# Weights, states and cached keys in contiguous runs, and four places for weights in a hybrid decoder step

## The reference, cut to what matters

```python
h = _rmsnorm(x, norm_mix_w)
z, xbc, dt_raw, q, kv_c, kv_s, kv_w, nsa_g, br_g = _split_proj(h @ w_in)       # 1024 x 8016 or so columns
y_ssm, conv_new, ssm_new = _mamba_branch(z, xbc, dt_raw, conv_prev, ssm_prev, ...)
o_attn, win_new = nsa_core(q, kv_c, kv_s, kv_w, gates)                         # compressed, selected, window
g = sigmoid(br_g)
merged = g[..., :D] * (y_ssm @ w_ssm_branch) + g[..., D:] * (o_attn @ w_attn_branch)
x = x + merged @ w_out
x = x + _peer_tokens(_rmsnorm(x, norm_ffn_w), peer_wq, peer_sub_keys, peer_u, peer_v)

# _causal_conv, inside _mamba_branch: width 4 over 3072 channels, with the last 3 inputs as state
xp = concatenate([conv_prev, xbc], axis=1)
conv_new = xp[:, -(CONV_WIDTH - 1):]
# _ssd: chunks of 128 tokens, a state of 32 heads x 64 x 128 carried from chunk to chunk and returned
# _peer: q = h @ peer_wq; scores against peer_sub_keys; 128 experts a token, one row of peer_u and of peer_v each
act = gelu(einsum('nd,nhkd->nhk', h, peer_u[experts]))
y = einsum('nhk,nhkd->nd', g * act, peer_v[experts])
```

## Time and profile before

| | before |
|---|---|
| time, three runs | 3235.7, 3231.45, 3214.28 us; median 3231.45 us |
| the profiled execution | 3234.93 us, of which the span of the profile is 3233.2 us |
| granted clock of TensorE, mean | 0.811 |
| busy time of TensorE (matmuls) | 2217.7 us, 69% of the span |
| busy time of VectorE | 1543.3 us, 48% |
| busy time of ScalarE | 616.9 us, 19% |
| busy time of GpSimd | 1492.6 us, 46% |
| read from HBM | 821.54 MB |

### The profile page before, as it was taken

How to read it: one execution, slowest core, us unless ns; L and a number is a source line. 1 busy time by engine, 2 the same in 40 slices (tenths; PEclk the granted TensorE clock), 3 DMA queues, 4 the chain that set the end, 5 groups by cost and what they waited for, 6 DMA issues and landing times. The chain is left out here.

```text
span 3233.2 us, 32111 instructions
## 1 busy us (share of the span) xinstructions
PE 2217.7 (69%) x11116; PEld 1403.4 (43%) x11116; DVE 1543.3 (48%) x3888; ACT 616.9 (19%) x1746; POOL 1492.6 (46%) x1509
## 2 busy tenths in 40 slices
PE   8999979869777678756688894653446777564044
PEld 7788846556555466422235362332114443111000
DVE  4410042276888751256520065998535665108720
ACT  3330053113331100013340012321001111000000
POOL 0200000053254664457754357657555665443775
PEclk9999969879978888877899996655668898777567
DMA  6234602437637997889989978968988998997998
GB/s 218 79 92 121 140 26 78 130 111 236 204 102 257 332 325 263 266 325 350 350 308 290 349 250 287 352 221 284 412 344 325 352 389 304 314 340 288 339 370 316
DMA packets 401016, 843.89 MB, mean 261 GB/s; under 512 B 71194, under 2 KB 236914, under 8 KB 398181
## 3 DMA queue, kind: packets, MB, share of 16 engines
q0 software_dynamic: 170912, 644.95, 54.6%
q1 hardware_dynamic: 229944, 196.89, 20.4%
HBM read 821.54 MB, written 24.33 MB: 262 GB/s over the span
## 5 line engine op out<-in xcount | busy, mean ns | idle before, releaser
L3314 POOL DMA_INDIRECT e_ring<-in_peer_u,e_idx x576 | 692.2, 1202 | 542.9 <-DVE e_dot L3463 267.4
L3463 DVE CUSTOM_DVE_ANT_0 e_ring<-e_ring,e_h 128x1024 f32<-128x1024 f32 x576 | 703.0, 1254 | 175.4 <-DMA e_ring<-in_peer_u,e_idx 82.4
L3314 POOL DMA_INDIRECT e_ring<-in_peer_v,e_idxT x576 | 583.4, 1013 | 440.3 <-PE ps L3381 178.1
L3381 PE MATMUL ps<-e_ring,e_wz 128*32 128x512 f32 x2304 | 361.5, 742 | 297.1 <-DMA e_ring<-in_peer_v,e_idxT 261.3
L3381 PEld LDWEIGHTS ps<-e_ring,e_wz 128*32 128x32 f32 x2304 | 76.8, 125 | 507.2 <-issue 502.4
L1672 POOL CAST ra_atf<-ra_at 128x32 f32<-128x32 uint32 x8 | 1.7, 211 | 259.7 <-DVE ra_hit L1665 259.7
L379 PE MATMUL ps<-hTb,wb 128*128 128x320 f32 x384 | 112.1, 447 | 1.9 <-DMA wb<-in_w_in 1.9
L1957 PE MATMUL ps<-ss_bsel,ss_xde 64*128 64x512 f32 x64 | 54.6, 947 | 63.1 <-DVE room L2007 27.5
L1004 PE MATMUL ps<-hTb,wb 128*128 128x320 f32 x256 | 77.3, 462 | 16.9 <-DMA wb<-in_w_in 9.6
L379 PEld LDWEIGHTS ps<-hTb,wb 128*128 128x128 f32 x384 | 73.7, 197 | 30.8 <-issue 2.9
L1507 DVE TENSOR_REDUCE apb_nmax<-ps 128x2 f32<-128x768 f32 (+1 forms) x32 | 34.9, 1089 | 105.9 <-PE ps L1431 55.3
(11 more groups left out here) (720 smaller groups left out, 4329.9 us busy)
## 6 DMA issues: line engine op xcount, KB each, us to landing
wb<-in_w_in SPq DMA_DIRECT2D x38, 1024.0 KB, 5.3
e_ring<-in_w_in SPq DMA_DIRECT2D x24, 1024.0 KB, 5.3
wb<-in_peer_wq SPq DMA_DIRECT2D x10, 1024.0 KB, 5.4
wb<-in_w_ssm_branch SPq DMA_DIRECT2D x9, 1024.0 KB, 6.1
e_ring<-in_peer_u,e_idx POOLq DMA_INDIRECT x576
e_ring<-in_peer_v,e_idxT POOLq DMA_INDIRECT x576
e_ring<-in_w_ssm_branch SPq DMA_DIRECT2D x7, 1024.0 KB, 5.8
wb<-in_w_in SPq DMA_DIRECT2D x24, 256.0 KB, 4.3
```

What stands on the lines that cost most here:

```text
L3314: nc.gpsimd.indirect_dma_start(out=self.ring[:, place % self.NR, :], out_offset=None, in_=k.peer_u if kind == "u" else k.peer_v, in_offset ...
L3381: last = nc.tensor.matmul(k.ps[32 * b:32 * b + 32, self.SUMS + i, :], self.wz[:, at:at + 32], self.ring[:, self.v_at[n] % self.NR, 512 * i ...
L3463: v.tensor_tensor_reduce(uu, uu, self.h[:, tile % 2, :], 1.0, 0.0, ALU.mult, ALU.add, self.dot[:, tile % 2, t:t + 1]).then_inc(self.dotted, 1)
```

## The change

The host lays out, before the launch, the weights of a group as pieces of 128 x 8 KB, contiguous in each partition (`weights`), the late stages' weights in pieces of 16 KB a partition (`late_weights`), the small vectors as columns (`columns`), the keys turned (`keys_turned`), the convolution's old state with channels on partitions (`conv_before`), the sample's states with the sequences side by side (`state_before`, 4 KB runs) and the window's cached rows page by page (`window_before`, 4 KB runs). The new states leave in the same layouts, and the host puts them into shape. In `conv` of group b the transposes of the states and their copies go, and `h` is stored as it is, in four quarters. In group b the weights have up to four places: the two of `wb`, `k.h` from `zgate` on, and `k.xs`, the sample's x, from `bs` on, once it is stored. `share_out` gives each piece the place, among those open to its part of the program, whose last piece is oldest.

The layout of the weights, and the places:

```diff
+def weight_pieces(np, w_in, w_ssm_branch, w_attn_branch, w_out, peer_wq):
...
+    def add(piece):
+        pieces.append(np.zeros((P, PIECE), np.float32))
+        pieces[-1][:, 0:piece.size // P] = piece.reshape(P, -1)
+    def block(w, c0, n):
+        return w[:, c0:c0 + n].reshape(-1, P, n).transpose(1, 0, 2)
...
+    for i in range(HPK // 2):
+        add(np.concatenate([block(w_in, COL_Q + (side * HPK + 2 * i + j) * HD, HD)
+                            for j in range(2) for side in range(KVH)], axis=2))
...
@@ class Weights
-                     for g, n in (("a", 2 + k.ex.NR // 2), ("b", 2))}
+                     for g, n in (("a", 2 + k.ex.NR // 2), ("b", 4))}
...
-        if g.first:
-            self.places += [ring[:, 2 * D * i:2 * D * i + 2 * D] for i in range(k.ex.NR // 2)]
+        self.places += [ring[:, 2 * D * i:2 * D * i + 2 * D] for i in range(k.ex.NR // 2)] if g.first else [k.h[:], k.xs[:]]
...
+    def share_out(self, g):
+        parts = [1 + CONV_DIM // 256, D_INNER // 256, KD // 2 * 3 + 4 + HPK // 2 + 1, KD // 2 * 2 + KD // 2 + PH]
...
+        free = [[0, 1], [0, 1, 2], [0, 1, 2, 3], [0, 1, 2, 3]]
+        opens = {2: [0, 1, 1, 3], 3: [0, 1, 2, 3]}
...
+            first = n - sum(parts[:part]) < 2
+            mine = range(self.slots) if g.first else [0, 1] if first else free[part]
+            slot = min(mine, key=lambda i: last[i])
...
+            self.opens.append(0 if g.first or slot < 2 else opens[slot][part])
@@ feed
-            old = n - self.slots
-            if old >= self.base + self.length:
+            old = self.before[n]
+            if old >= self.base + self.length or self.opens[n] > self.part[self.base]:
                 return
             if old >= self.base:
                 sp.wait_ge(*self.used(old - self.base))
-            for part, src in self.pieces[n]:
-                sp.dma_start(part(self.places[n % self.slots]), src).then_inc(self.sem[n % self.slots], 16)
+            width = self.pieces[n]
+            sp.dma_start(self.places[self.slot[n]][:, 0:width],
+                         self.k.weights[n][:, 0:width]).then_inc(self.sem[self.slot[n]], 16)
```

The stages:

```diff
@@ stage_conv
-        TURNS = F if g.sample else B_TILES
...
+                sp.dma_start(before.rearrange("p f b t -> p (f b t)"), k.conv_before).then_inc(state_in, 16)
             k.w.feed(sp)
...
-                if g.sample:
-                    if f == 0:
-                        pe.wait_ge(state_in, 32)
-                    last = nc.tensor.transpose(k.ps[:, f % 2, N:N + 24], ends(f, 24), k.ident[0:24, 0:24])
...
-                if g.sample:
-                    pe.wait_ge(tailed, f + 1)
-                    last = nc.tensor.transpose(k.ps[0:27, b, 3 * P:4 * P], tail[:, f % 2, :], k.ident[:])
...
-                    last = a.copy(ends(f, 27), k.ps[0:27, b, 3 * P:4 * P])
...
-                    last = a.copy(cin_s[:, f % 2, :, 0:3], src[:, N:N + 24].rearrange("p (b t) -> p b t", b=NB))
+                    if f == 0:
+                        act.wait_ge(state_in, 16)
+                    last = a.copy(cin_s[:, f % 2, :, 0:3], before[:, f])
@@ stage_ssd
-                        last = nc.tensor.transpose(k.ps[:, q, i * P:i * P + P], h[:, f * P:f * P + P], k.ident[:])
...
-                sp.wait_ge(h_copied, 4)
...
+                for gr in range(GROUPS):
+                    sp.wait_ge(updated, U - GROUPS + gr + 1)
+                    sp.dma_start(k.new_ssm_prompt[:, channels(gr)], h[:, channels(gr)]).then_inc(h_stored, 16)
+                sp.wait_ge(h_stored, 16 * GROUPS)
@@ stage_branch
                 sp.dma_start(k.xs_dram, k.xs[0:NS, :]).then_inc(x_kept, 16)
+                k.w.feed(sp, k.w.first_in(3))
+                sp.wait_ge(x_kept, 16)
             k.w.feed(sp)
-            if g.sample and not which:
-                sp.wait_ge(x_kept, 16)
@@ stage_query
-            sp.dma_start(*((sk[:], keys) if g.first else (skT[:], k.skT_dram))).then_inc(sk_in, 16)
+            sp.dma_start(skT[:], k.keys_turned).then_inc(sk_in, 16)
...
-                    if g.first:
-                        turn_keys()
@@ stage_sample_state
-                sp.dma_start(h0[f % NH0], view(k.state_ssm, f)).then_inc(h0_in[f % NH0], 16)
+                sp.dma_start(h0[f % NH0], k.state_before[f].rearrange("p (b n) -> p b n", b=NB)).then_inc(h0_in[f % NH0], 16)
@@ stage_sample_branch
-                for dst, part in load_w(wp[i % 2], w, i):
-                    sp.dma_start(dst, part).then_inc(wp_in[i % 2], 16)
+                sp.dma_start(k.room[i % 2], k.late_weights[first + i]).then_inc(wp_in[i % 2], 16)
```

More of the change, by code:

```diff
@@ L440, in _ @@
                     project(f)
[L441 removed]
+                if 1 <= f <= B_TILES:
                     turn(f - 1)
@@ L743, in _ @@
                     ex.pe(2 * u + 1)
-            if g.sample:
-                pe.wait_ge(updated, U)
-                pe.wait_ge(y_half, U)
-                for q in range(4):
-                    for i in range(4):
-                        f = 4 * q + i
-                        last = nc.tensor.transpose(k.ps[:, q, i * P:i * P + P], h[:, f * P:f * P + P], k.ident[:])
-                    last.then_inc(h_turned, 1)
         @block.scalar
@@ L1804, in _ @@
                     a.copy(qT[:, i % 2, :], k.ps[:, i % 2, 0:NP]).then_inc(q_copied, 1)
-                if i == 1 and g.first:
-                    for q in range(HC // 4):
-                        act.wait_ge(sk_turned, q + 1)
-                        a.copy(skT[:, 4 * q:4 * q + 4, :],
-                               k.ps[:, 2 + q % 2, :].rearrange("p (i n) -> p i n", i=4)).then_inc(sk_copied, 1)
                 if i:
```

292 lines of the change are left out of this document (132 added, 160 removed).

## The result

The changed kernel takes 3093.6 us (median of four runs, 3088.7 to 3099.5) against 3227.6 us of the kernel before in the same comparison (3214.3 to 3235.7): 0.9589 of it, with an interval of 0.955 to 0.9629. It is 134 us faster. The profiled execution took 3088.7 us, with a span of 3086.9.

The account below looks back on a forecast made before the run. TensorE's 74.7 us of waits for weight pieces in group b were the target; VectorE bound `zgate` and `state`, bytes `sbs`. Terms summed to 79 us off the profiled 3234.9, 3156, less 3.5 over the median: 3152 us, range 3105 to 3190.

Parts of the forecast that it names:

- Four stages with weight waits: Group b's `bs`, `qk`, `kv`, `ba`: -20, -16, -4 and -13 us as weight waits fall; `query` another -4.
- TensorE alone would need 143.9 - 32 = 112: In `bs`: TensorE's time once about 32 us of weight waits are taken from the stage.
- TensorE's own floor is 96: In `ba`: the 112.4 us stage less about 16 us of waits; the stage was forecast at 99 us.
- a rival of 0.17: Whole kernel, "More than forecast": higher TensorE clock without stalls and late weights give 35 to 40 us more, 3115; chance 0.17.
- The choice of 124: Time forecast for `bs`, -20 us (bounds -12 to -30), among alternatives of 127, 123 and 116.
- With four, the first piece of `bs` that is not there at its start goes into `xs`: In `bs`: four places allow earlier issue, so about 32 us of waits fall if the DMA engines can deliver.
- `kv`: -4 forecast: In `kv` of group b: its 3.8 us of TensorE waits for weight pieces go.
- The convolution: -7 forecast: `conv` of group b: 0.28 us less per tile, a third of tiles giving nothing, 4.5; last turns and stores 2.5.
- Late stages and window: -5 forecast: Late weights' longer runs -4 us (bounds +8 and -25), gathers' turn coming later; state and window keys -1.
- Group a: -4 forecast: Keys turned by the host -3 us in `query` of a; fewer small transposes and loads in the first stage -1.
- the bytes bind, not the packets: Rival: `bs` and `ba` keep their time, weight waits becoming waits for gathered rows; 46 us gained, 3185; chance 0.15.
- Slower: Rival: long packets delay gather packets, which cost 3.4 us a MB instead of 2.72; kernel at 3277; chance 0.03.

Follow-up runs that it names:

- two_shifted: Changed kernel with long runs and two places, and 12 gathers moved from `bs` to `ssd`: 3017.7 us, 0.9556 of before.
- stall_ba: Changed kernel with three idle stretches of TensorE put into `ba` of group b: the stage grew by 12.9 us from 88.94; no total given.
- short_two: Changed kernel with short runs, one DMA a piece, and two places for weights: 3091.1 us, 0.9806 of before.
- orig_two: Changed kernel with both groups' weights loaded as before from the stored matrices, and two places: 3122.3 us, 0.9912 of before.
- orig_four: Changed kernel with both groups' weights loaded as before from the stored matrices, but its four places: 3063.0 us, 0.9732 of before.

## Why the forecast fell short

**Four stages with weight waits: 57 us forecast for them and `query`, 94 measured** (28.2 in `bs`, 12.9 `kv`, 21.1 `qk`, 23.5 `ba`, 8.7 `query`). This is the largest part of the miss. TensorE's idle time in them fell by 65 us; that half of the step is near the forecast. Its busy time fell by 29 us, for the same instructions. The failing step is "TensorE alone would need 143.9 - 32 = 112" and, in `ba`, "TensorE's own floor is 96": both took the stage less its waits as a floor, though the busy time in it had been run at 0.84 and 0.92 of the clock. `ba` went under that floor, to 88.9, at 1.00, and also under the 95 to 98 put down for its DMA engines, which need 0.99 x 88.9 = 88. In `bs` the clock did not set the length: there the bytes bind (a share of 1.01; with 12 gathers fewer the stage took 104.3 us in `two_shifted`), and the next paragraph has its 8 us. The term stood in the text, with almost the right size (0.1 of 260 us), but as a rival of 0.17 and not in the sum; and the measured time lies under that rival's 3115 too. `stall_ba` shows that the term belongs with the stalls. The mean time of a product with `w_ssm_branch` says it in one row, before and after:

```profile
L1012 PE MATMUL ps<-xnatb,wb 128*128 128x256 f32 x256 | 66.9, 427 | 24.2 <-DMA wb<-in_w_ssm_branch 24.2
```

```profile
L961 PE MATMUL ps<-xnatb,wb 128*128 128x256 f32 x128 | 28.1, 379 | 0.0
```

**`bs` at its floor of bytes.** The choice of 124 was wrong by its own alternatives: with gathers at the price of `sbs` the sum had given 116, and 115.7 was measured, at 404 GB/s and a share of 1.01. The DMA queues in `bs` of the changed kernel, from 1075 to 1188 us in its second profile, answer to the earlier trace rows:

```profile
q0 software_dynamic: 8734, 31.81, 71.0%
q1 hardware_dynamic: 1879, 13.69, 30.0%
```

Gathers cost 0.71 x 113 / 31.81 = 2.52 us a MB, the 2.51 of `sbs`, instead of 2.72; weights 0.30 x 113 / 13.69 = 2.48 instead of 3.37. The forecast had 2.70 for the latter, from a stretch that it called light; it was not, since gathers took 63.8% of the engines' time beside the 35.5%. The limit of about 358 GB/s that the Trainium skill states (DMA: Bandwidth & Descriptors, Where 436 GB/s comes from) did not bind: the trace shows 404 over the whole stage.

**What cured the waits.** "With four, the first piece of `bs` that is not there at its start goes into `xs`" named the places as the cure and the runs as what pays for the bytes. The time would have been the same with two places. The first trace gives no landing times for the pieces of `bs`, but its waits hint at them: up to 8.8 us behind the products on one piece, 66.9 / 8 = 8.4 us, so an estimate of some 17 us under way from these two rows. Whether longer runs would shorten that was the question to ask first.

**`kv`: -4 forecast, -12.9 measured.** Missed was a stage change, 6.6 us, during which TensorE waited for SyncE's queue with the quarters of the q pieces; it stood in the waits of `qk` and not in any weight's name. The forecast had named the full queue, but only for the 17.6 us behind it, and there it was wrong: in `short_two`, with one DMA for each q piece and two places, TensorE still waited 14.5 us for pieces in `qk`. What took that wait away was a place to fetch ahead into, or the long runs.

**The convolution: -7 forecast, -3.0 measured.** The period of a tile fell by 0.43 us (5.07 to 4.64) rather than 0.28, but only in tiles that VectorE's work for the experts does not delay. The step "in about a third of the tiles" was too small a discount: the trace after has only five steps from tile to tile near 4.64 us, where the one before has 14 near 5.07. **End of `ssd`:** -6 forecast, -7.4 measured; the last of the four stores is issued just ahead of 957 and `zgate` starts at 959.14. **`state`, `zgate`:** 0, as forecast.

**Late stages and window: -5 forecast, about 18 measured** by the comparison in the same rounds (18.9 in the first pair of profiles). "Hidden or given back" was largely wrong: the sample's `attn`, for which no term stood, gave the most. **Group a: -4 forecast, -12.9 in the first pair of profiles, -7.5 in the second**, of which keys, vectors and the faster `kv` and `bs` are the steady part.

The rival "the bytes bind, not the packets" fell: `bs` carries 400 GB/s with random gathers beside it, though 31 of the 74.7 us came back as waits for gathered rows. "Slower" fell too: gather packets became cheaper in `bs`, not dearer.

## What to carry to other kernels

Where a transfer must beat a fixed stretch of work, look at its time from issue to landing in the company it keeps; a longer run can do what more buffers would, and the second cure then adds nothing. When a wait of TensorE goes, count the busy time beside it at the clock it will have then, not at the one it had, and count the stalls that go as well as their length. And a stage change that waits for the queue of the issuing engine belongs to the cost of many small DMAs.

## What the runs showed of the hardware

- Three stalls of TensorE of 2.4 to 2.6 us in a stage of 89 us lowered its mean granted clock from 1.00 to 0.95 and made the same 448 matmuls 5.3 us longer. Behind the first stall the granted clock was 0.53 for 2.1 us, 0.64 for the next 2.0 and then 1.00.
- A 1 MB weight piece in 512-byte and 1 KB runs took 5.3 to 24.0 us to land beside gathers of 4 KB rows in the kernel before (15.2 in the median), 5.1 to 24.3 with `orig_two` (12.8), in 8 KB runs 6.8 to 9.3 us (8.0) with two places and 7.8 to 11.9 (8.5) with four; without gathers, in group a, the short ones took 5.3 to 5.8 in the median.
- With four such short-run pieces under way the issue of one held SyncE for up to 19.5 us (`orig_four`), against 0.37 us with two (`orig_two`).
- Random gathers and weights together moved 404 GB/s over 116 us, with 16 DMA engines at 1.01; the same gathers beside short runs 342 at 0.99, with four places in both.
- The same kernel differed by 2.2 to 2.5% between chips (3227.6 and 3149 to 3159 us), most of it in stages that gather: `attn_prompt` of b took 272 us on one and 241 on another.
